# A two-block transformer kernel on one core: buffers 128 bytes further up, the RWKV inverse on its own blocks, one scan, and a new order of the dense parts

## What is computed

```python
def frame_step(S, inp):
    r_t, w_t, k_t, v_t, kk_t, a_t = inp
    sa = jnp.einsum('bhvk,bhk->bhv', S, -kk_t)
    S = (S * w_t[:, :, None, :] + sa[..., None] * (kk_t * a_t)[:, :, None, :]
         + v_t[..., None] * k_t[:, :, None, :])
    return S, jnp.einsum('bhvk,bhk->bhv', S, r_t)
...
u = lax.conv_general_dilated(u, conv_w[:, None, :], window_strides=(1,), padding=((CONV_WIDTH - 1, 0),), ...)
```

## Time and profile before

| what | value |
|---|---|
| median of 3 runs | 2250.59 us |
| profiled execution, its own time | 2251.5 us |
| its span (first to last instruction) | 2249.7 us |
| TensorE busy | 2103.1 us, 93% |
| VectorE busy | 1188.6 us, 53% |
| ScalarE busy | 800.9 us, 36% |
| GpSimd busy | 736.3 us, 33% |
| mean granted TensorE clock | 0.971 of full speed |
| one middle tile of the RWKV loop | 80.56 us |

### The profile page before, as it was taken

How to read it: one execution, slowest core, us unless ns; L and a number is a source line. 1 busy time by engine, 2 the same in 40 slices (tenths; PEclk the granted TensorE clock), 3 DMA queues, 4 the chain that set the end, 5 groups by cost and what they waited for, 6 DMA issues and landing times. The chain is left out here.

```text
span 2249.7 us, 34219 instructions
## 1 busy us (share of the span) xinstructions
PE 2103.1 (93%) x13936; PEld 1650.2 (73%) x13936; DVE 1188.6 (53%) x1963; ACT 800.9 (36%) x1292; POOL 736.3 (33%) x347
## 2 busy tenths in 40 slices
PE   6898989999999999988999999999999998999997
PEld 5775567887788888766777776676777787888885
DVE  6427775333652342738778668777813456523322
ACT  2336655223332232443333333333333434322321
POOL 0221021444344444542232133223223443444442
PEclk9989999999899999999999999999999999999998
DMA  7531011533232333231101111101122322233331
GB/s 263 187 128 38 30 47 66 175 116 95 70 98 94 94 96 97 82 106 41 34 32 46 34 34 45 43 29 44 44 85 98 122 94 76 93 94 98 99 95 57
DMA packets 51450, 186.51 MB, mean 83 GB/s; under 512 B 5728, under 2 KB 6880, under 8 KB 50784
## 3 DMA queue, kind: packets, MB, share of 16 engines
q1 hardware_dynamic: 47520, 174.49, 23.8%
q10 hardware_dynamic: 3776, 9.83, 1.2%
HBM read 178.01 MB, written 6.29 MB: 82 GB/s over the span
## 5 line engine op out<-in xcount | busy, mean ns | idle before, releaser
L680 POOL TENSOR_TENSOR wlo<-raw,whi 128x1024 fp32r<-128x1024 f32 x266 | 644.5, 2424 | 1337.8 <-ACT whi L1295 1337.7
L765 PE MATMUL psum<-ah,whi 128*128 128x512 f32 x1288 | 538.2, 418 | 26.5 <-POOL wlo L680 16.0
L766 PE MATMUL psum<-ah,whi 128*128 128x512 f32 x1288 | 512.0, 398 | 0.0
L767 PE MATMUL psum<-ah,wlo 128*128 128x512 f32 x1288 | 511.6, 397 | 0.0
L1295 ACT ACTIVATE whi<-raw 128x1024 fp32r<-128x1024 f32 x266 | 280.2, 1054 | 367.2 <-PE psum L767 304.0
L765 PEld LDWEIGHTS psum<-ah,whi 128*128 128x128 f32 x1288 | 247.5, 192 | 98.2 <-POOL wlo L680 26.1
L767 PEld LDWEIGHTS psum<-ah,wlo 128*128 128x128 f32 x1288 | 247.2, 192 | 54.3
L766 PEld LDWEIGHTS psum<-ah,whi 128*128 128x128 f32 x1288 | 248.3, 193 | 43.5 <-issue 0.2
L2005 DVE SCALAR_TENSOR_TENSOR x<-upad,vec,x 128x512 f32<-128x512 f32 x240 | 211.5, 881 | 5.2
L765 PE MATMUL psum<-hidden,whi 128*128 128x512 f32 x536 | 213.0, 397 | 0.0
L766 PE MATMUL psum<-hidden,whi 128*128 128x512 f32 x536 | 212.7, 397 | 0.0
(11 more groups left out here) (340 smaller groups left out, 2916.8 us busy)
## 6 DMA issues: line engine op xcount, KB each, us to landing
raw<-in_w SPq DMA_DIRECT2D x322, 512.0 KB, 3.5
x<-in_x SPq DMA_DIRECT2D x1, 2048.0 KB, 7.9
x_kept<-x ACTq DMA_DIRECT2D x1, 2048.0 KB, 9.7
ao_kept<-ao ACTq DMA_DIRECT2D x8, 256.0 KB, 2.0
aof<-ao_kept ACTq DMA_DIRECT2D x1, 2048.0 KB, 10.8
x<-x_kept ACTq DMA_DIRECT2D x1, 2048.0 KB, 8.4
out<-x SPq DMA_DIRECT2D x1, 2048.0 KB, 6.3
lwt<-in_lw ACTq DMA_DIRECT2D x8, 128.0 KB, 2.0
```

The source lines that it names most:

```text
L680: pool.tensor_tensor(wlo[:, s % NHL, :], raw_of(SPLITS[s]), whi[:, s % NHL, :].bitcast(F32), ALU.subtract).then_inc(lo_done, 1)
L765: pe.matmul(dst, wh, h_, start=first, stop=False)
L766: pe.matmul(dst, wh, l_, start=False, stop=False)
L767: return pe.matmul(dst, wl, h_, start=False, stop=last)
```

## The change

Three things are changed together.

**Addresses.** A buffer `to_line` of 32 floats (128 bytes) is put behind `modg`. In the built program `raw`, `whi`, `wlo`, `ah` and `tmp` begin at multiples of 256 bytes in each partition, before and after (`whi` at 54016, `ah` at 70400). All buffers that are allocated behind `modg` move. `oh` and `hidden0` begin at 117888 before, which is 128 bytes past a multiple of 256, and at 118016 after, which is a multiple of 256; `cqh`, `yh`, `hidden1` and `aoh` go from 150656 to 150784 in the same way, and `coh` as `oh`. The small buffers of the recurrence (`ma`, `mr`, `ix`, `iy`, `ip` and on to `st`) go the other way, from a multiple of 256 to 128 past one.

**The small steps.** `ix` and `iy` hold, of each pair of chunks, only the 64 columns of a chunk's own block. `inv` transposes 64 x 64 blocks, the lower ones by a matmul with the identity. What ScalarE and VectorE move of them is 128 x 256, not 128 x 512. `mr` and `kr` are made by one VectorE instruction each, not four, and the scan over 512 tokens by one with a mask, not by eight. `opv`, `rr` and `opa` are one step for both heads, with their matmuls in turn. The reciprocals stand as steps of their own (`kkinv`, `gninv`).

**The order.** Products ahead have two parts of 4 x 3 matmuls, not four of 2 x 3, and they stand at named places. Where none is named, small steps follow each other. The taps are spread anew: 15 in the levels and behind `tav` and `rr`, and one behind each of the six `st`.

```diff
 def tile_ahead(j):
-    k, r, v, g = (parts(what, 4) for what in (("rkv", j, 1), ("rkv", j, 0), ("rkv", j, 2), ("glu", j, 1)))
-    return (k + [("lw2", j)] + r[:2] + [("mix", j, 1), ("scan", j)] + r[2:] + [("la2", j)] + v[:2] + [("mix", j, 0), ("kk", j)]
-            + v[2:3] + [("lg2", j)] + v[3:] + [("kkss", j)] + g[:1] + [("mix", j, 2)] + g[1:2] + [("kkb", j)] + g[2:3] + [("bonus", j)]
-            + g[3:] + [("at", j)])
+    k, r, v, g = (parts(what, 2) for what in (("rkv", j, 1), ("rkv", j, 0), ("rkv", j, 2), ("glu", j, 1)))
+    return {("ip", 1): k[:1] + [("conv", 1)], ("iy", 1): k[1:] + [("lw2", j), ("conv", 3)],
+            ("iy", 2): r[:1] + [("mix", j, 1), ("conv", 3)], ("inv", 2): [("scan", j)],
+            ("iy", 3): r[1:] + [("la2", j), ("conv", 2)], ("inv", 3): [("mix", j, 0)],
+            ("iy", 4): v[:1] + [("kk", j)], ("inv", 4): [("lg2", j)], ("ip", 5): [("kkss", j)],
+            ("iy", 5): v[1:] + [("kkinv", j), ("conv", 2)], ("tav", 0): g[:1] + [("mix", j, 2), ("kkb", j), ("conv", 2)],
+            ("rr", 0): g[1:] + [("bonus", j), ("at", j), ("conv", 2)]}
...
         for c in range(1, NCK - 1):
-            out += [("st", j, c)] + last[1 + c:2 + c]
+            out += [("st", j, c), ("conv", j, 1)] + last[1 + c:2 + c]
         out.append(("ost", j))
...
         modg = sb("modg", [P, 2 * KT])
+        sb("to_line", [P, 32])
...
-            ix, iy, ip = both("ix", TT * P), both("iy", TT * P), both("ip", TT * CH)
+            ix, iy, ip = both("ix", TT * CH), both("iy", TT * CH), both("ip", TT * CH)
...
-                    for t in range(TT):
-                        mm = pe.transpose(b[:, t * P:t * P + P], iy[hh][:, t, :], eye)
+                    for t, own in own_chunks:
+                        dst, src = b[own, t * CH:t * CH + CH], iy[hh][own, t, :]
+                        mm = pe.matmul(dst, src, eye[own, own], start=True, stop=True) if own.start else pe.transpose(dst, src, eye[own, own])
...
                     for t in range(TT):
-                        mm = pe.matmul(psum[RN * hh:RN * hh + RN, OBANK, t * P:t * P + P], vtk[:, t, hh * RN:hh * RN + RN],
-                                       kr[hh][:, t, :], start=t == 0, stop=False, skip_group_check=True)
+                        for hh in range(2):
+                            mm = pe.matmul(psum[RN * hh:RN * hh + RN, OBANK, t * P:t * P + P], vtk[:, t, hh * RN:hh * RN + RN],
+                                           kr[hh][:, t, :], start=t == 0, stop=False, skip_group_check=True)
...
-                    for c in range(NCK):
-                        cols = slice(c * CH, c * CH + CH)
-                        last = dve.tensor_tensor_scan(cw[:, cols], ones[:, 0:CH], sw[:, cols], 0.0, ALU.mult, ALU.add)
...
+                    last = dve.tensor_tensor_scan(cw[:, :], later, sw[:, :], 0.0, ALU.mult, ALU.add)
                     last.then_inc(cw_ready, 1)
...
-                    for t in range(TT):
-                        last = dve.tensor_tensor(both_chunks[f[2]][:, t, :].rearrange("p (c n) -> p c n", c=2),
...
+                    emptied_by(dve.tensor_tensor(both_chunks[f[2]].rearrange("p t (c n) -> p t c n", c=2),
```

More of the change, by code:

```diff
@@ L155, in rwkv_order, with behind @@
     for j in range(KT):
-        ahead = tile_ahead(j + 1) if j + 1 < KT else [f for m in range(GATES_IN) for f in parts(("gate2", m), 4)]
+        ahead = tile_ahead(j + 1) if j + 1 < KT else gates_ahead()
         last = parts(("glu", j + 1, 0), KT) if j + 1 < KT else []
[L159 to L164, removed]
+        def behind(step, level=0):
+            return [(f[0], j, f[1]) if f[0] == "conv" else f for f in ahead.get((step, level), [])]
         out += [("tok", j, 0), ("mb", j, 0), ("tok", j, 1), ("mb", j, 1), ("iy0", j, 0), ("iy0", j, 1)]
@@ L171, in rwkv_order @@
             out.append(("gnv", j - 1))
-        out += [("akv", j, 0), ("akv", j, 1), ("inv", j, 1, 0), ("opv", j, 0), ("opv", j, 1)]
+        out += [("akv", j, 0), ("akv", j, 1), ("inv", j, 1, 0), ("opv", j)]
+        if j:
+            out.append(("gninv", j - 1))
         for lv in range(1, LEVELS + 1):
@@ L181, in rwkv_order @@
             if lv < LEVELS:
[L182 to L185, removed]
+                out += [("inv", j, 0, lv), ("inv", j, 1, lv)] + behind("inv", lv)
+        out += [("tav", j, 0), ("tav", j, 1)] + behind("tav") + [("rr", j)] + behind("rr")
+        out += [("opa", j)] + last[:1] + [("pt", j, 0), ("pt", j, 1)] + last[1:2] + [("qq", j, 0), ("qq", j, 1)]
+        out += [("re", j + 1)] if j + 1 < KT else []
         for c in range(1, NCK - 1):
-            out += [("st", j, c)] + last[1 + c:2 + c]
+            out += [("st", j, c), ("conv", j, 1)] + last[1 + c:2 + c]
         out.append(("ost", j))
     gates = [f for m in range(GATES_IN, 16) for f in parts(("gate2", m), 1)]
-    behind = [[("gnm", KT - 1)], [("gnv", KT - 1)], [("gnb", KT - 1), ("gnend", KT - 1)], [("aoput", KT - 1)], [("aoload", KT - 1)], []]
-    behind += [[("aosplit", k), ("aosplit", k + 1)] for k in range(0, KT, 2)]
+    then = [[("gnm", KT - 1)], [("gnv", KT - 1), ("gninv", KT - 1)], [("gnb", KT - 1), ("gnend", KT - 1)], [("aoput", KT - 1)], [("aoload", KT - 1)], []]
+    then += [[("aosplit", k), ("aosplit", k + 1)] for k in range(0, KT, 2)]
     for m, f in enumerate(gates):
-        out += [f] + (behind[m] if m < len(behind) else [])
+        out += [f] + (then[m] if m < len(then) else [])
     return out
@@ L405, in rwkv_constants @@
     own = lambda m: np.where(i < CH, m[:, :CH], m[:, CH:])
-    out = [own(i < t), same & (i <= t)]
+    out = [own(i < t), same & (i <= t), np.broadcast_to(np.arange(S) % CH > 0, (P, S))]
     for lv in range(LEVELS + 1):
@@ L542, in build_program @@
         usig, og, tf = tmp[:, 0, :], tmp[:, 1, :], tmp[:, 2, :]
-        strict, incl = rw[:, 0:CH], rw[:, CH:CH + P]
-        level = [rw[:, CH * (3 + lv):CH * (4 + lv)] for lv in range(LEVELS + 1)]
-        own_eye = rw[:, CH * (4 + LEVELS):CH * (5 + LEVELS)]
-        heads = rw[:, CH * (5 + LEVELS):CH * (5 + LEVELS) + P]
+        strict, incl, later = rw[:, 0:CH], rw[:, CH:CH + P], rw[:, CH + P:CH + P + S]
+        rest = rw[:, CH + P + S:]
+        level = [rest[:, CH * lv:CH * (lv + 1)] for lv in range(LEVELS + 1)]
+        own_eye = rest[:, CH * (1 + LEVELS):CH * (2 + LEVELS)]
+        heads = rest[:, CH * (2 + LEVELS):CH * (2 + LEVELS) + P]
         with ExitStack() as at:
@@ L1166, in _ @@
                     for t, own in own_chunks:
[L1167 removed]
+                        mm = pe.matmul(b[own, t * CH:t * CH + CH], ma[hh][own, t, :], ix[hh][own, t, :], start=True, stop=True)
                 elif kind == "iy":
```

78 lines of the change are left out of this document (35 added, 43 removed).

## The result

The changed kernel takes 2426.3 us (median of 4 runs, 2424.39 to 2430.51) against 2248.8 us for the kernel before on the same chip. The ratio is 1.079, with a 95% interval of 1.0767 to 1.0814: 177 us slower, where I had forecast 2251 us and a range up to 2266 us. All of it is in the RWKV loop; the stages behind it got shorter.

The account below looks back on a forecast made before the run. TensorE was taken as the bound, in the loop its list plus late hand-overs from VectorE and ScalarE. 2251.5 - 15.5 (addresses) + 14.5 (loop) + 2.3 (clock) = 2252.8 us, 2251.9 on the median's basis, given as 2251; range 2235 to 2266.

Parts of the forecast that it names:

- The step that failed: In the levels behind `lw2`, TensorE has only `inv` to do, taken as 1.0 us, while `ix` is queued on ScalarE.
- the clock: In the RWKV loop, TensorE's lower clock in half of the seven tiles, where two had it before: +2.3 us.
- rival 2: Idle stretch lowers the clock to 1.2 GHz in all seven tiles, twice as long: 18 us more, 2269 us; chance 0.12.
- The addresses: In the dense stages, moving operands starting at multiples of 256 bytes make matmuls issue faster: 15.5 us off.
- The start of a tile: Eleven taps ahead of `upad` delay `mb.0` and `gnm`, so `ip.0.1` begins 4.8 us later; bounds 3.5 and 6 us.
- The levels: Fewer dense parts, alternating heads and shorter waits, less 3.0 us of new waits: a gain of 3.4 us per tile.
- the wait behind `lw2`: In the levels, ScalarE's table load and `sw` hold up `ix` of the next `inv`: 1.4 us of new wait.
- The state chain: A tap in each step's loop makes it 1.345 us, not 1.15; five steps cost 0.95 us per tile.
- Tile 0 and the last tile: Tile 0 has no eleven taps ahead: -3 us; the last has the late start and a longer chain: +3.5 us.
- (1): In the loop, levels gain 5.5 us per tile or taps hide as well: 2237 or 2218 us; chance 0.22 together.
- (3): In the dense stages, the addresses do nothing because something else sets the rate: 15.5 us more, 2267 us; chance 0.07.
- (4): GpSimd's `wlo` holds VectorE at a tap or the scan: 1.5 us more per tile, 2262 us; chance 0.09.

Follow-up runs that it names:

- e2: The changed kernel with all sixteen 64x64 products of an inv as matmuls with the identity, no transposes; 2288.2 us, ratio 1.0145 to the kernel before.
- e6: e2 with five extra matmuls on TensorE that change no output, run behind the stall at tok.3; 2291.5 us, ratio 1.0177 to the kernel before.
- e1: The kernel before with only the 128-byte shift of buffers (`to_line`), same instructions in the same order; 2237.5 us, ratio 0.9929.
- e12: e10 with two taps fewer behind kk in level 4, one more behind ip of level 1 and one more behind tav; 2231.6 us, ratio 0.9921.
- e3: The changed kernel with the four transposes of a head's inv together, then its four matmuls; 2328.4 us, ratio 1.0328 to the kernel before.
- e5: e2 with the ten left-over taps moved from ahead of upad to behind steps of the levels; 2258.2 us, ratio 1.0034 to the kernel before.
- e7: The changed kernel with the order of before (tile_ahead, taps, parts) and inv by matmuls alone; 2213.5 us, ratio 0.9840 to the kernel before.
- e10: e5 with one tap behind rr in place of four and two behind tav in place of three; 2230.8 us, ratio 0.9926 to the kernel before.
- e8: e7 but with the changed kernel's inv, transposes and matmuls alternating; 2358.7 us, ratio 1.0479 to the kernel before.
- e11: e7 with the inverse of before (full transposes) and eight scans; 2218.9 us, ratio 0.9871 to the kernel before.

## Why the prediction was wrong

**The step that failed** is one that it took for granted: TensorE "has only `inv` to do (1.0 us)". The diff turns the four full transposes of a head into eight products that change between two kinds at every instruction, and I gave them the duration of the old ones without looking for a row on it. There was none: no step of the kernel before goes back and forth between transposes and matmuls at every instruction. Measured, both heads take 3.42 us at the full clock where matmuls alone take 1.08, so 94 us for the 40 pairs of the program. With what the clock adds, the alternation is 138 us by the times and 145 by the ratios (changed kernel against e2), out of a loss of 177. No rival had it. It was an operation that the trace did not show; a bound from above was missing, and with it the range.

**The second term mis-sized is the clock.** I took 2.3 us for the whole program, from the two tiles of the earlier trace rows, and 21 us in rival 2. (That rival's 2269 us counts again what the two tiles of before had already lost, 3 us; its own terms give 2267.) In e2, where nothing alternates, the low clock came behind the stall in all seven tiles, for 10 to 14 us, and cost 5.1 us in the tile compared (e2 against e6); for seven tiles that is an estimate of 36 us. Rival 2 was thus the right mechanism with too short a stretch. The slow tile of the earlier trace rows had its low stretch over the same kind of small steps; its window, and `akv` in it and in the tile behind it:

```profile
1259.90:1263.50 3.60, 3.60 (x41) 3.14 (x41) 0.55 (x3) 2.63 (x6) 0.00 (x0) 0.53 0.02 5
```

```profile
1260.03 1.97 PE L1162 MATMUL psum<-vtk,ka 64*64 64x64 f32 x32
1342.09 1.15 PE L1162 MATMUL psum<-vtk,ka 64*64 64x64 f32 x32
```

It cost 1.5 us for 3.4 us at the lower clock, which is no less for its length than 5.1 for 14. I doubled that length; behind the stall it is three to four times as long in e2, and 17 to 21 us in the changed kernel, which has the further low stretches on top. What the clock costs the changed kernel in all, no run has by itself. The Trainium skill (TensorE: Matmul & The Clock Gate, HAM oscillation), which I had put on record, says that idle gaps between bursts throttle the clock again and again. The traces agree behind the stall, in seven tiles of seven; the stretches without a stall are another matter, and are taken up in the last section. Weighing that rule against two rows of before was the wrong way round.

**The addresses:** forecast 15.5 us, measured 16 by the ratio (e1). Right, in rate and in sum.

**The start of a tile:** forecast +4.8 us. In e2 it is +8.8 (20.65 against 11.86 us to the first `ip`); less 5.1 for the clock it is +3.7, within the bounds of 3.5 to 6. Eleven taps of 8.6 us (said 8.5), `upad` behind them and the stall of 4.8 us at `tok.3` are all as written.

**The levels:** forecast -3.4 us. From the first `ip` to `pt` e1 takes 56.4 us, and e12, whose levels have no taps late, 53.6: -2.8. The terms were near: twelve matmuls in a piece take 2.95 us against 2 x 1.58, and the wait behind `lw2` is 1.40. In e2 it is only -1.3, as a part ran at the low clock.

**The state chain:** forecast +0.95 us. The end of a tile from `st` on takes 8.6 us in place of 8.0: +0.6.

**Tile 0 and the last tile:** forecast -3 and +3.5. Tile 0 itself takes 77.6 us in e2 against 80.8 in e1, -3.2 and as written. But its start comes at 1006.3 us in e2 and at 999.8 in e1, and in the other kernels from e3 on between 1002.9 and 1008.2 (one profiled execution of each), so up to the start of tile 1 e2 is 3.3 us behind. I had nothing for that, and no run takes it apart. The last tile of e2 takes 11.8 us more (84.5 against 72.7, to the last product of `ost`), with 22 us at the lower clock in place of 3. That term was too small by a factor of three.

**The other rivals.** (1), that the levels give more or the taps hide, is refuted for this kernel. (3), that the addresses do nothing, is refuted by e1. (4), GpSimd holding VectorE at a tap, is real but smaller than its 1.5 us: most taps take 0.75 to 0.79 us, and three or four of the 30 in a tile take 1.4 to 2.8 us, each while an instruction of GpSimd runs. That was so before as well. The taps of a tile add up to 26.4 us in the changed kernel and 25.9 before, and TensorE waits for none of the slow ones there. In e5 it matters more: the four taps ahead of `pts` take 4.03 us, not 3.10. On its own the order of the change costs about 70 us, 69 to 75 with the taps as they are (e2 against e7, by ratios and by times) and 17 to 19 us with the taps spread (e10). What part of these 17 each thing in it has (the waits behind the moved taps, the clock behind those, a longer tile 0 and last tile) was not taken apart.

## What to carry to other kernels

Price each new form of instruction by how far apart its records start, next to its actual neighbours, and if the trace has no such row, bound it from above by the worst sequence that the trace has; a transpose that takes a matmul's place in the middle of matmuls is a new form. Here a stall of TensorE cost itself, and then what stood behind it ran at half the clock, so a burst of foreign work ahead of a chain of small steps was dear twice. Spreading it was better, but at each place one has to ask what is emptied behind it. And when a change of six parts comes out slower, split it before dropping it: here the parts without the order, and with one expression changed, are 1.6% faster than the kernel before.

## What the runs showed of the hardware

Alternating 64x64 transposes and matmuls costs 3.42 us for sixteen, against 1.08 us for sixteen matmuls with the identity that compute the same, and 1.89 us if the kinds are grouped by head. Why one change is dear, no run shows. The Trainium skill (TensorEngine Tiling (Array Packing), Restrictions) says that column tiling disables transpose mode for FP32 inputs. That could make each transpose here a special case, but the rows speak against a slow transpose as such: the whole of e3's sixteen, eight transposes among them, takes 1.89 us.

The clock fell in e8 without a stall, while transposes alternated with matmuls; with matmuls alone in the same places (e7) and with full transposes (e11) it stayed at 1.00 through nearly all of the loop. The Trainium skill (TensorE: Matmul & The Clock Gate, PE-mode transpose) says that a transpose doesn't count as busy in the way a matmul does. e8 agrees with that; e11, whose inverses are all transposes but only a third as long, neither confirms nor refutes it. e3 narrows it: it has the same eight transposes in each `inv` as the changed kernel, grouped, and behind the first low stretch of a tile the clock falls again in only one of its six middle tiles, against two to four times in each tile of the changed kernel. So the number of the transposes alone does not do it. Whether their share of the time or the gaps between the alternating records lower the clock stays open.

The rate of an fp32r product goes by where its moving operand begins: 0.2267 us for 512 columns at a multiple of 256 bytes (`ah` before, `hidden` and `yh` in the changed kernel, `hidden` in e1), and 0.2322 to 0.2333 us at 128 bytes past one (`yh` and `hidden` before). e1 moves the buffers and changes nothing else. Only these two offsets were run, and the fast starts (70400, 118016, 150784) are all odd multiples of 256, so whether 256 bytes is the period, no run shows.
